# A ring of expert weight pieces with 20 places in place of 18, two of its pieces loaded ahead of the others

## The reference

```python
def _moe(h, w_router, router_bias, w_expert_gate_up, w_expert_down, w_shared_gate_up, w_shared_down):
    ...
    scores = jax.nn.sigmoid((t @ w_router).astype(jnp.float32))
    sel = scores + router_bias.astype(jnp.float32)
    ...
    _, ei = lax.top_k(sel, TOP_K)
    ...
    gu = jnp.einsum('td,edf->etf', t, w_expert_gate_up)
    g, u = jnp.split(gu, 2, axis=-1)
    act = jax.nn.silu(g) * u * combine.T[:, :, None]
    routed = jnp.einsum('etf,efd->td', act, w_expert_down)
    sg, su = jnp.split(t @ w_shared_gate_up, 2, axis=-1)
    shared = (jax.nn.silu(sg) * su) @ w_shared_down
    return (routed + shared).astype(jnp.float32).reshape(bsz, length, d)
```

## Time and profile before

| | us |
|---|---|
| median of 3 runs (847.36 to 848.35) | 847.51 |
| span of the profiled execution | 846.6 |
| PE busy | 795.1 (94%) |
| DVE busy | 381.6 (45%) |
| ACT busy | 236.0 (28%) |
| POOL busy | 20.9 (2%) |

### The profile page before, as it was taken

One profiled execution on the slowest core, in us unless ns is written; L12 is line 12 of the kernel. 1 busy time (PEld: TensorE's weight loads), 2 busy tenths in 40 slices (PEclk: granted clock), 3 DMA queues, 4 the chain that ended last, 5 costly groups with the idle time before them and its releaser, 6 DMA issues.

```text
span 846.6 us, 12875 instructions
## 1 busy us (share of the span) xinstructions
PE 795.1 (94%) x5234; PEld 543.4 (64%) x5234; DVE 381.6 (45%) x773; ACT 236.0 (28%) x400; POOL 20.9 (2%) x22
## 2 busy tenths in 40 slices
PE   4999999999999999999999999699999999799974
PEld 1779897999999999855355455254555745355212
DVE  1176999879987664673333222021221211122114
ACT  2163747244354443231112111021111111011002
POOL 1000010000000100200000000000000000000000
PEclk9999999999999999999999999799999999999988
DMA  8999897423524399889999999999999999999995
GB/s 320 387 377 338 285 341 259 169 101 105 195 101 138 112 324 366 325 344 392 366 418 419 414 419 416 418 416 420 413 419 408 416 416 416 416 417 419 415 414 198
DMA packets 81221, 284.71 MB, mean 336 GB/s; under 512 B 5256, under 2 KB 12040, under 8 KB 64520
## 3 DMA queue, kind: packets, MB, share of 16 engines
q1 hardware_dynamic: 80664, 282.55, 85.7%
q10 hardware_dynamic: 496, 1.30, 0.4%
HBM read 280.67 MB, written 3.16 MB: 335 GB/s over the span
## 4 chain that ended last, share of the span: by engine, by line
PE 61%; SPq 20%; DMA 11%; DVE 3%; issue 2%; ACT 2%; POOL 0%; DVEq 0%; POOLq 0%
SPq L627 17%; PE bank L2105 12%; PE bank L2161 6%; PE bank L1720 6%; PE bank L1722 6%; PE bank L1725 6%; DMA chunk<-in_w_expert_down 5%; PE bank L1989 3%; PE bank L1782 3%; PE bank L2012 3%; PE bank L1706 3%; PE bank L1764 3%; DMA chunk<-in_w_expert_gate_up 2%; PE bank L1667 2%; DMA ring<-in_w_out 2%
## 5 line engine op out<-in xcount | busy, mean ns | idle before, releaser
L2105 PE MATMUL bank<-chunk,xg 128*64 128x512 f32 (+2 forms) x1024 | 201.4, 621 | 19.6 <-DMA chunk<-in_w_expert_gate_up 19.3
L2105 PEld LDWEIGHTS bank<-chunk,xg 128*64 128x64 f32 (+2 forms) x1024 | 62.6, 130 | 152.2 <-issue 135.8
L2161 PE MATMUL bank<-chunk,act_t 128*64 128x512 f32 (+2 forms) x480 | 97.4, 613 | 2.1 <-DMA chunk<-in_w_expert_down 2.1
L1519 DVE SCALAR_TENSOR_TENSOR act_r<-bank,w_slot,sil 128x256 f32<-128x256 f32 x26 | 12.6, 484 | 181.4 <-ACT sil L988 181.4
L1531 DVE TENSOR_TENSOR y_lo<-bank,y_hi 128x512 fp32r<-128x512 f32 x52 | 35.9, 691 | 73.7 <-ACT y_hi L1001 73.7
L988 ACT ACTIVATE sil<-bank 128x256 f32<-128x256 f32 x26 | 10.0, 384 | 210.2 <-PE bank L2105 210.2
L1083 DVE TENSOR_TENSOR ring_lo<-ring,ring_hi 128x1024 fp32r<-128x1024 f32 x44 | 52.9, 1220 | 23.6 <-ACT ring_hi L770 23.4
L2161 PEld LDWEIGHTS bank<-chunk,act_t 128*64 128x64 f32 (+2 forms) x480 | 30.0, 129 | 48.7 <-issue 47.9
L1001 ACT ACTIVATE y_hi<-bank 128x512 fp32r<-128x512 f32 x52 | 30.9, 597 | 102.0 <-PE bank L2161 98.0
L1143 DVE SCALAR_TENSOR_TENSOR conv<-upad,dw,conv 128x256 f32<-128x256 f32 x120 | 52.8, 512 | 0.0
L770 ACT ACTIVATE ring_hi<-ring 128x1024 fp32r<-128x1024 f32 x44 | 44.4, 1054 | 27.4 <-PE bank L1746 12.6
(11 more groups left out here) (316 smaller groups left out, 1201.5 us busy)
## 6 DMA issues: line engine op xcount, KB each, us to landing
chunk<-in_w_expert_gate_up SPq DMA_DIRECT2D x128, 1024.0 KB, 20.9
chunk<-in_w_expert_down SPq DMA_DIRECT2D x63, 1024.0 KB, 22.5
ring<-in_w_in SPq DMA_DIRECT2D x16, 2048.0 KB, 10.1
ring<-in_w_ada SPq DMA_DIRECT2D x12, 2048.0 KB, 8.8
ring<-in_w_proj_hgrn SPq DMA_DIRECT2D x2, 2048.0 KB, 8.0
ring<-in_w_out SPq DMA_DIRECT2D x2, 2048.0 KB, 14.0
ring<-in_w_proj_conv SPq DMA_DIRECT2D x1, 2048.0 KB, 7.8
chunk<-in_w_shared_gate_up SPq DMA_DIRECT2D x2, 1024.0 KB, 23.5
```

Source lines behind the costliest of these rows:

```text
L2105: ins = mm(bank[2 + b][row:row + width, :], xg[:, k, c:c + width], w[:, k % 4, :], start=(k == 0), stop=(k == KD - 1))
L2161: ins = mm(out[row:row + width, :], act_t[:, c, row:row + width], w[:, c, h * 512:(h + 1) * 512], start=(c == 0), stop=(c == 1))
```

## The change

The ring gets 20 places. The two new ones stand first in `PLACES`, at -16 and -8 KB, so below the point from which offsets count; the other 18 keep their offsets and their order, two indices later. Room for them comes from the scratch of dynamic DMAs, which shrinks from 16 KB to 128 bytes; `BASE` goes from 16512 to 16640. The static pieces are still 18. Pieces 0 and 1 go to the two new places and are loaded right behind block "zb1" in the first stage. Pieces 2 to 17 take the places that pieces 0 to 15 had, behind the same waits. The places that had pieces 16 and 17 (56 and 96 KB) now get pieces 18 and 19, the first two ranked ones, which wait for no earlier piece; the second of them has the wait that piece 17 had. From piece 20 on the wait is for the piece 20 numbers before.

```diff
-NCHUNK = 18
+NCHUNK = 20
+EARLY_CHUNKS = 2
...
-PLACES = [152, 160, 168, 112, 120, 88, 16, 24, 80, 144, 32, 40, 48, 0, 8, 72, 56, 96]
+PLACES = [-16, -8, 152, 160, 168, 112, 120, 88, 16, 24, 80, 144, 32, 40, 48, 0, 8, 72, 56, 96]
 EXTRA_PLACES = 12
-FINAL_PLACES = (15, 16, 17)
+FINAL_PLACES = (17, 18, 19)
...
-BASE = 16512
+SCRATCH = 128
+BASE = 16 * KB + SCRATCH + 128
...
+                if name == "zb1":
+                    for number in range(EARLY_CHUNKS):
+                        load_fixed(number)
             filled(sp, "gb1", 1)
...
-            for number in range(NCHUNK):
-                if number == 3:
+            for number in range(EARLY_CHUNKS, 3 * FIXED):
+                if number == 5:
                     sp.wait_ge(o_ready, 4)
                     sp.wait_ge(s_g2_kept, 16)
...
-                if number == 13:
+                if number == 15:
                     released(sp, "wo1")
-                if number == 17:
-                    sp.wait_ge(s_x1_kept, 16)
-                    sp.wait_ge(x1_sq, 5)
-                    sp.wait_ge(g_done, 5)
                 load_fixed(number)
...
                         number = CHUNK_NO[step, part, item]
-                        freed(number - NCHUNK)
+                        if number < NCHUNK:
+                            if number == NCHUNK - 1:
+                                sp.wait_ge(s_x1_kept, 16)
+                                sp.wait_ge(x1_sq, 5)
+                                sp.wait_ge(g_done, 5)
+                        else:
+                            freed(number - NCHUNK)
...
-    nc = bacc.Bacc("TRN2", target_bir_lowering=False, num_devices=1)
+    nc = bacc.Bacc("TRN2", target_bir_lowering=False, num_devices=1, dynamic_dma_scratch_size=SCRATCH)
```

More of the change, by code:

```diff
@@ L545, in load_block, with load_part, load_fixed @@
                 sp.dma_start(tile_of(name), dict(blocks)[name]).then_inc(s_w[place[name]], 16)
+            def load_part(number, part, e):
+                src = dn_src[e] if part == 2 else gu_src[e][:, 4 * part:4 * part + 4, :]
+                dst = (dn_tile if part == 2 else gu_tile)(place_of(number))
+                sp.dma_start(dst, src).then_inc(s_chunk[place_of(number)], 16)
+            def load_fixed(number):
+                step, part, item = CHUNK_AT[number]
+                load_part(number, part, FIRST_FIXED + sum(ITEMS_OF[:step]) + item)
             for x, dst in loads_small[0::2]:
@@ L564, in _ @@
             load_block("wo0")
[L566 to L570, removed]
             evacuated(sp, "st", 3)
             sp.dma_start(new_state[0, 0].rearrange("a h k v -> k (a h) v"), s_new[:, :, :]).then_inc(s_state, 16)
-            def load_fixed(number):
-                step, part, item = CHUNK_AT[number]
-                load_part(number, part, FIRST_FIXED + sum(ITEMS_OF[:step]) + item)
             def mod_row(m, s):
                 return A["mod_rows"].rearrange("(k s) (m c) -> s m k c", s=NS, m=2)[s:s + 1, m].broadcast_to([P, KD, P])
-            for number in range(NCHUNK):
-                if number == 3:
+            for number in range(EARLY_CHUNKS, 3 * FIXED):
+                if number == 5:
                     sp.wait_ge(o_ready, 4)
@@ L589, in _ @@
                         sp.dma_start(shift_row[:, s, :].rearrange("p (k c) -> p k c", k=KD), mod_row(0, s)).then_inc(s_s0, 16)
-                if number == 5:
+                if number == 7:
                     sp.wait_ge(ob_used, 4)
-                if number == 6:
+                if number == 8:
                     load_block("wo1")
                     released(sp, "ph1")
-                if number == 10:
+                if number == 12:
                     released(sp, "wo0")
-                if number == 12:
+                if number == 14:
                     filled(sp, "wo1", 0)
-                if number == 13:
+                if number == 15:
                     released(sp, "wo1")
-                if number == 17:
-                    sp.wait_ge(s_x1_kept, 16)
-                    sp.wait_ge(x1_sq, 5)
-                    sp.wait_ge(g_done, 5)
                 load_fixed(number)
```

## The result

The changed kernel takes 834.99 us (median of 4 runs, 833.25 to 837.35) against 847.93 us of the kernel before: a ratio of 0.9844, 95% interval 0.9822 to 0.9865. That is 13 us faster, where the prediction had 5 us (842.5 us, range 841.2 to 845.3). The sign of the prediction holds and its size is far off: about 8 us more came than it could explain. The profiled execution took 835.81 us with a span of 834.0 us, 12.6 us less than the span before.

A forecast was written before the change was run, and what follows sets the result against it. It took the expert stage to be bound by a full DMA queue at 416 GB/s: span 846.6 - 5.04 (two pieces), other terms 0, = 841.6, plus 0.9 from span to median, gives 842.5 us; range 841.2 to 845.3.

The forecast's parts named there:

- What bounds the kernel: Expert stage, 406 to 828 us: bound by a full DMA queue at 416 GB/s, PE having 21 us to spare.
- Two pieces less in the full stage: Expert stage: two of 195 pieces move earlier into idle queue time, making every later landing 5.04 us earlier.
- the first hole: Idle queue time at 372 to 376 us, 3.14 us idle; 3.0 us of the gain was expected here.
- the second hole: Idle queue time at 402 to 406 us, 2.72 us idle; expected to absorb 2.0 us and keep about 0.7.
- The early pair in the first stage: Pieces 0 and 1 behind zb1: 5.3 us of bytes fit 5.4 us of holes; cost 0 us.
- Smaller scratch, shifted base: Scratch of dynamic DMAs and BASE: no use of the scratch seen in the trace; effect taken as 0 us.
- The bound below: Largest gain allowed for the two pieces: 5.04 plus the 1.5 us shortage between the holes, -6.5 us.
- Slower: Rival, each of 175 ranked issues: SP's dynamic issue becomes dearer with the 128-byte scratch; 860 us, chance 0.04.
- Half absorbed: Rival: the pair fills the hole at 372 us but not that at 402; gain 3.0 to 3.4 us, 844.3 us, chance 0.11.
- Deeper queue: Rival: the shortage between the two holes goes too, up to 1 us more; 841.5 us, chance 0.06.
- No change: Rival: early pair stalls PE 5.3 us in the first stage, or PE bounds the expert stage; 847.5 us, chance 0.05.

The follow-up runs named there:

- e2: Changed kernel with all tiles 128 bytes higher, so 128 past a multiple of 256 (b_router and mod moved down): 843.61 us, 0.9937 of the kernel before.
- e6: Changed kernel with all tiles 64 bytes higher, so 64 past a multiple of 256: 843.92 us, 0.9951 of the kernel before.
- e11: The changed kernel run again with no edit: 835.39 us, 0.9841 of the kernel before.
- e3: Kernel before with only the scratch of dynamic DMAs cut from 16 KB to 128 bytes: 848.67 us, 0.9999 of the kernel before.
- e1: Kernel before with only BASE changed from 16512 to 16640, 18 places and 16 KB scratch kept: 840.67 us, 0.9905 of the kernel before.
- e7: Kernel before with BASE 16576, so tiles start 192 bytes past a multiple of 256: 849.02 us, 1.0010 of the kernel before.
- e8: Changed kernel with down weights reordered, one 8 KB run per partition in place of two of 4 KB: 833.59 us, 0.9820 of the kernel before.
- e4: Changed kernel with ranked piece 18 also waiting for the end of PE's first pass: 837.40 us, 0.9859 of the kernel before.
- e5: Changed kernel with pieces 0 and 1 issued behind piece 14, not in the first stage: 834.50 us, 0.9841 of the kernel before.
- e9: Kernel before with 128-byte scratch and BASE 16384, so tiles start at multiples of 4096, 18 places: 840.03 us, 0.9896 of the kernel before.

## Why the prediction was wrong

**What bounds the kernel: right.** The stage is bound by a full DMA queue, and its end moved with the last landing, 12.6 us of 12.6 us. PE followed: from 505 to 548 us it waits 4.6 us for pieces (10.0 before), and 7.7 + 1.1 = 8.8 us after that (14.2 before, all its waits for pieces counted), so it is still not the bound. That 4.6 lies near the 5.0 predicted is luck: the faster rate is in it, and in e2, at the rate that the prediction had, these waits are 3.4 + 4.0 = 7.4 us. The tail is 17.9 us, as predicted.

**Two pieces less in the full stage: right in size.** e2 has it alone, 5.3 us (3.5 to 7.2) against 5.04, and e6 has it once more, 4.2 us (2.6 to 5.8). The split is off. The prediction had 3.0 us in the first hole, 2.0 in the second and nothing between them. By e2's rows, at 417 GB/s, idle time fell by 1.9 us in the first, 1.4 between them and 1.7 in the second: 5.0 in all. In the changed kernel the issues went at 372.1 and 373.3 us in place of 371.4 and 372.6, and the second hole kept 1.4 us in place of 0.7. How much falls to each hole also moves from profile to profile: in e11, the same kernel, SP issues from 371.0 us on, and the holes have 326 and 289 GB/s in place of 227 and 270. The later landings moved by two pieces all the same, as there was idle time enough in front of 406 us.

**The early pair in the first stage: right.** PE has no wait for a transfer from 20 to 320 us in the kernel after. The hole behind zb1 is the one that it fills (after, columns of rows 2; the earlier trace rows had 133 GB/s there):

```profile
114.00:118.00 4.00, 4.00 (x38) 2.86 (x31) 4.00 (x12) 2.06 (x3) 0.00 (x0) 1.00 1.03 432
```

**"Smaller scratch, shifted base ... I take 0": the step that failed.** It looked at the scratch, found no reader of it, and stopped, which e3 confirms for the scratch. The shift of BASE by 128 bytes, written into the same line, was given no thought. It is worth 8.1 us (e1), more than the two places. The same error stands once more in the sum: the 416 GB/s of the earlier trace rows were taken for what the DMA engines can do, a constant, when they were what they did with the tiles 128 bytes off. The stretch of 422 us at 416 GB/s is 175.6 MB; at 424 GB/s it takes 414 us, 8 us less. So the term was 0, and should have been -8. The bound below, -6.5 us, rested on the same constant, and so the range had no room for it.

The Trainium skill has a page that bears on this, and the prediction did not use it: a descriptor that starts off a multiple of 256 bytes begins with a transaction from the multiple below, whose unused bytes still cost beats (DMA: Bandwidth & Descriptors, How a descriptor splits into AXI transactions). The page speaks of bytes that are fetched, and in these runs only the end in SBUF, which is written, was shifted. e1 and e2 show that a start off the multiple costs something there too. The cost doesn't grow with the bytes below the start: 64, 128 and 192 bytes cost the same (e6, e2, e7). What fits all of them is one transaction more for each descriptor, since any start off the multiple gives one more, but no run here shows transactions.

**The rivals.** "Slower", by a dearer issue with the small scratch, is refuted by e3. "Half absorbed" had 3.0 to 3.4 us and the second hole left as it was. The times alone don't settle it: e2's interval begins at 3.5 us, but e6's has these values in it. The rows do: the second hole has 312 GB/s in e2 where it had 133, and the passes that wait for pieces begin 5.0 to 5.2 us earlier. "Deeper queue" was half right: the shortage between the holes did go (415 GB/s in e2 in place of 392), but as part of the 5 us and not on top of them; and what made the changed kernel faster than 841.5 us is the rate, which rose in the kernel with 18 places as well (e1). "No change" is out by the result, and both of its reasons by the waits: none for a transfer in the first stage, and 8.8 us of waits for pieces after 548 us.

**What stays open.** The runs moved all tiles together. DVE and ACT were busy for 381.6 and 236.2 us after, 381.6 and 236.0 before, and PE, which still waits for pieces, 793.0 against 795.1, so the gain is not in what the engines read and write there. That it is the transfers' end in SBUF is argued from that and from the packet records, but no run shifted the pieces' places alone. Only 64, 128 and 192 bytes off were run, in the direction from HBM to SBUF. And why e8 brought only half of what was expected is told by the DMA share alone.

## What to carry to other kernels

When a queue is full for half of the time, the rate at which it runs is a term of the sum like any other: ask what would change it, above all the start of the tiles in SBUF (here a multiple of 256 bytes; 128 bytes off cost 1.9% of the rate with runs of 4 and 8 KB and 5% with 2 KB) and the number of runs of bytes. A line of a diff that only moves addresses must be priced on its own, and an experiment that shifts one constant would have been the cheapest one here. Two more places in this ring were worth the idle time in front of the full stage that they filled, and no more; in which of two idle stretches the early pieces were moved made no difference.

## What the runs showed of the hardware that I had not expected

- Tiles that start 64, 128 or 192 bytes past a multiple of 256 cost each run of bytes of an incoming transfer some 4 to 5 ns, whatever its length: 8 KB 314.4 against 309.6 ns, 4 KB 163.3 against 159.3, 2 KB 88.5 against 84.0. The stage runs at 416 to 417 GB/s in every kernel off the multiple (before, e2, e3, e6, e7) and at 423 to 424 in those on it with the same weights' layout (e1, e4, e5, e9, e11 and the changed kernel). A multiple of 4096 is no better.
- The DMA share did not show it: 1.02 in both. Here a share near 1 told that the engines were busy, not that they were at their best.
- The scratch of dynamic DMAs can shrink from 16 KB to 128 bytes for a kernel whose dynamic transfers are issued by SP, at no cost (0.9999, 0.9985 to 1.0014).
- With the queue full, issuing a piece takes SP longer: 0.34 us at 373.30 and 4.11 us at 708.12 in the changed kernel. A gate and up piece lands 20.2 us after its issue there (median), the time in which about eight pieces land at 424 GB/s.
